# Front of a decoder-layer kernel: weight chunks begin beside x on a second queue, and the 80-column product moves behind the first group

## The reference

```
h    = rms_norm(x, attn_norm_g)
proj = h @ w_in                       # (256, 2048) @ (2048, 11344)
(q_sb, k_sb, v_sb, q_ds, k_ds, v_ds, q_ix, k_ix, w_ix, g_sb, g_ds) = split(proj)
```

## Time and profile before

| what | value |
|---|---|
| median of 3 runs | 1457.61 us |
| the profiled execution's own time | 1458.54 us |
| its span, first to last instruction | 1456.6 us |
| PE busy | 1444.3 us (99%) |
| DVE busy | 1025.4 us (70%) |
| ACT busy | 799.1 us (55%) |
| GpSimd busy | 431.1 us (30%) |
| moved by DMA | 272.12 MB, mean 187 GB/s |

### The profile page before, as it was taken

The page is one execution under the profiler, slowest core; times in us unless marked ns, Lnnn a source line. Parts: engine busy times, 40 slices in busy tenths (PEclk is TensorE's granted clock), DMA queues, the critical chain, the costliest instruction groups (busy, mean ns, idle before and its releaser), DMA issues.

```text
span 1456.6 us, 24290 instructions
## 1 busy us (share of the span) xinstructions
PE 1444.3 (99%) x7640; PEld 1236.5 (85%) x7640; DVE 1025.4 (70%) x1352; ACT 799.1 (55%) x1107; POOL 431.1 (30%) x486
## 2 busy tenths in 40 slices
PE   8999999999999999999999999999999999999998
PEld 6888888888888888888888888888888888788887
DVE  6545455886655556775557778777777778899987
ACT  6544445565766756665455454545554545455553
POOL 1100000323222223450005556655556555200000
PEclk9999999999999999999999999999999999999999
DMA  7666665666555555575666666666666665576664
GB/s 244 194 182 187 182 179 172 188 178 183 147 171 164 153 168 176 188 245 183 192 175 187 188 190 186 181 192 199 190 187 180 194 189 187 173 242 205 196 209 145
DMA packets 130493, 272.12 MB, mean 187 GB/s; under 512 B 10784, under 2 KB 10816, under 8 KB 130192
## 3 DMA queue, kind: packets, MB, share of 16 engines
q1 hardware_dynamic: 129664, 269.12, 60.2%
q0 software_dynamic: 464, 2.42, 0.5%
q10 hardware_dynamic: 320, 0.01, 0.0%
HBM read 269.42 MB, written 2.10 MB: 186 GB/s over the span
## 4 chain that ended last, share of the span: by engine, by line
PE 95%; DVE 2%; POOL 1%; issue 1%; DMA 1%; ACT 0%; DVEq 0%; ACTq 0%; POOLq 0%; SPq 0%
PE bank L1640 94%; DVE lo L1239 1%; PE bank L1689 0%; POOL u L1604 0%; DMA rows_in<-in_attn_norm_g 0%; DMA raw<-in_w_down 0%; POOL conv L1607 0%; PE bank L1823 0%; DVE conv L1193 0%; DVE y L1329 0%; PE bank L1863 0%; POOL conv L1621 0%; DVE leftb L1308 0%; DVE hT L907 0%; ACT hi L820 0%
## 5 line engine op out<-in xcount | busy, mean ns | idle before, releaser
L882 DVE TENSOR_TENSOR lo<-raw,hi 128x1024 fp32r<-128x1024 f32 (+1 forms) x423 | 545.2, 1293 | 314.3 <-ACT hi L511 313.5
L511 ACT ACTIVATE hi<-raw 128x1024 fp32r<-128x1024 f32 (+1 forms) x423 | 445.5, 1055 | 408.2 <-PE bank L1640 403.4
L1640 PE MATMUL bank<-h2T,hi 128*128 128x512 f32 x1408 | 483.3, 394 | 0.0
L1640 PE MATMUL bank<-h2T,lo 128*128 128x256 f32 x1408 | 376.6, 278 | 0.0
L1640 PEld LDWEIGHTS bank<-h2T,hi 128*128 128x128 f32 x1408 | 257.9, 188 | 53.6
L1640 PE MATMUL bank<-hT,hi 128*128 128x512 f32 (+1 forms) x784 | 273.3, 394 | 0.7 <-DVE lo L882 0.7
L1640 PEld LDWEIGHTS bank<-h2T,lo 128*128 128x128 f32 x1408 | 264.5, 188 | 7.8
L1640 PE MATMUL bank<-hT,lo 128*128 128x256 f32 (+1 forms) x784 | 214.7, 284 | 0.0
L1640 PE MATMUL bank<-hi,hT 128*128 128x512 f32 x640 | 198.0, 390 | 0.0
L1604 POOL TENSOR_TENSOR u<-u,rms_row 128x256 f32<-128x256 f32 x88 | 121.0, 1375 | 239.7 <-DVE u L1183 220.7
L1640 PE MATMUL bank<-hi,ffT 128*128 128x512 f32 x576 | 177.6, 390 | 2.1 <-DVE lo L1239 2.1
(11 more groups left out here) (223 smaller groups left out, 1574.9 us busy)
## 6 DMA issues: line engine op xcount, KB each, us to landing
raw<-in_w_in SPq DMA_DIRECT2D x176, 512.0 KB, 3.6
raw<-in_w_up SPq DMA_DIRECT2D x176, 512.0 KB, 3.8
raw<-in_w_down SPq DMA_DIRECT2D x88, 512.0 KB, 4.3
raw<-in_w_branch SPq DMA_DIRECT2D x32, 512.0 KB, 3.6
raw<-in_w_out SPq DMA_DIRECT2D x32, 512.0 KB, 3.8
y<-in_x SPq DMA_DIRECT2D x4, 512.0 KB, 6.7
y<-in_x POOLq DMA_DIRECT2D x1, 2048.0 KB, 9.4
out<-y SPq DMA_DIRECT2D x8, 256.0 KB, 3.6
```

The lines of the kernel that those rows point to most:

```text
L511: act.activation(hi[s][:, 0:width], raw[s][:, 0:width], ACT.Copy)\
L882: dve.tensor_tensor(lo[s][:, 0:width], raw[s][:, 0:width], hi[s][:, 0:width].bitcast(f32), ALU.subtract)\
L1640: return pe.matmul(o, l, r, start=start, stop=stop, skip_group_check=True)
```

## The change

1. SP issues no x and no 80-column loads. It begins with the first large chunks; its waits are satisfied for the first four, since DVE, PE and ACT raise `lo_done`, `w_used` and `hi_done` by 4 in advance (and SP itself `w_landed`).
2. x comes on ACT's queue, in four column quarters of two loads each (256 KB a load, 8 loads), issued behind the gain. The positions are loaded by GpSimd.
3. The first group's product starts when k tiles 0 and 1 of x and the first chunk are there. The other transposes of x are inserted behind chunks 0 to 5, two k tiles at a time, and so are their copies on ACT and DVE, the four squares on ACT and the five parameter transposes.
4. The 80 columns get own buffers (`wtail`, `wtail_hi`, `wtail_lo`), are loaded by GpSimd in four pieces, converted in two halves at (g, j) = (0, 6) and (0, 7), and multiplied after chunk 7 into bank B[2], behind `spread_rms`. The small work behind it moves to later j.
5. `rows_in` is no longer zeroed (only the rows that are loaded are read). The identity is ready before the other patterns, PE waits for it alone, and it does 11 idle transposes in place of 14.

The diff, cut to what these points touch:

```diff
@@ SP
-            for half in range(2):
-                cols = slice(half * BLOCK, (half + 1) * BLOCK)
-                for t in range(TH):
-                    sp.dma_start(y[:, t, cols], x[0, t * P:(t + 1) * P, cols])\
-                        .then_inc(x_in[2 * half + t], 16)
...
+            for s in range(SLOTS):
+                sp.sem_inc(w_landed[s], 16)
@@ ACT
-            act.wait_ge(rows_zero, 1)
+            prime(act, relu_done, tok_done, tok_done, *[hi_done] * C_ROWS)
             act.dma_start(rows_in[0:KT, 0, :], attn_norm_g.rearrange("(t p) -> t p", p=P))\
                 .then_inc(small_in, 16)
+            for q in range(4):
+                for t in range(TH):
+                    cols = slice(q * GRP, (q + 1) * GRP)
+                    act.dma_start(y[:, t, cols], x[0, t * P:(t + 1) * P, cols])\
+                        .then_inc(x_in[2 * q + t], 16)
...
+            transposed_hi(hT, 0, 0, range(0, 2))
             split(C_ROWS)
+            transposed_hi(hT, 0, 0, range(2, 4))
             split(C_ROWS + 1)
             split(C_ROWS + 2)
+            transposed_hi(hT, 0, 0, range(4, 6))
...
+                            if g == 0 and j < 5:
+                                transposed_hi(hT, 0, 0, range(2 * j + 6, 2 * j + 8))
+                            if g == 0 and 1 <= j < 5:
+                                squares((j - 1) // 2, (j - 1) % 2)
...
+                            if (g, j) == (0, 6):
+                                tail_split(0)
                                 norm_rstd(0)
+                            if (g, j) == (0, 7):
+                                tail_split(1)
+                                act.wait_ge(rstd_done, 1)
+                            if (g, j) == (1, 0):
+                                rms_copy(0)
+                            if (g, j) == (1, 1):
+                                act.wait_ge(angle_done, 1)
+                                act.activation(trig[:, :, :, :], ang[:, :, :, :], ACT.Sin)\
+                                    .then_inc(sin_done, 1)
+                                act.wait_ge(tail_prod, 1)
+                                act.activation(tailT[0:TAIL, :], B[2][0:TAIL, S:2 * S], ACT.Copy)\
+                                    .then_inc(tailT_half, 1)
@@ DVE
+                        if not index and (g, j) == (0, 5):
                             dve.wait_ge(const_sel, 2)
                             mean_squares(0, 2)
+                        if not index and (g, j) == (0, 6):
+                            tail_split(0)
+                        if not index and (g, j) == (0, 7):
+                            tail_split(1)
                             rms_diagonal(0)
...
@@ GpSimd
-            pool.memset(rows_in[:, :, :], 0.0).then_inc(rows_zero, 1)
...
+            for c in range(4):
+                rows = w_in[c * 4 * P:(c + 1) * 4 * P, TAIL_AT:TAIL_AT + TAIL]
+                pool.dma_start(wtail[:, 4 * c:4 * c + 4, :],
+                               rows.rearrange("(k p) c -> p k c", p=P)).then_inc(tail_in, 16)
@@ PE
-            pe.wait_ge(const_sel, 2)
-            keep_warm(14)
+            pe.wait_ge(const_sel, 1)
+            keep_warm(11)
...
+            x_transposes(range(0, 4))
...
+            def tail_product():
+                pe.wait_ge(tail_lo, 2)
+                for kt in range(KT):
+                    mm(B[2][0:TAIL, :], wtail_hi[:, kt, :], hT[:, kt, :], kt == 0, False)
+                    i = mm(B[2][0:TAIL, 0:S], wtail_lo[:, kt, :], hT[:, kt, 0:S], False,
+                           kt == KT - 1)
+                i.then_inc(tail_prod, 1)
...
+                        if not index and g == 0:
+                            pe.wait_ge(xT_lo, CK * (j + 1))
                         rows_chunk(C_ROWS + g * CPG + j + 1 + 2 * CPG * b, j % SLOTS, hT,
...
+                            if g == 0 and j < 6:
+                                x_transposes(range(2 * j + 4, 2 * j + 6))
+                            if (g, j) == (0, 4):
+                                other_params()
+                            if (g, j) == (0, 7):
+                                spread_rms(0)
+                                tail_product()
+                            if (g, j) == (1, 1):
                                 pe.wait_ge(tailT_done, 1)
```

More of the change, by code:

```diff
@@ L274, in hybrid_layer @@
         w_used = sem("w_used")
-        x_in = [sem(f"x_in{i}") for i in range(2 * TH)]
+        x_in = [sem(f"x_in{i}") for i in range(4 * TH)]
         pos_in = sem("pos_in")
@@ L543, in squares @@
             def squares(half, t):
-                act.wait_ge(x_in[2 * half + t], 16)
+                for q in (2 * half, 2 * half + 1):
+                    act.wait_ge(x_in[2 * q + t], 16)
                 act.activation(junk[:, t, half * BLOCK:(half + 1) * BLOCK],
@@ L554, in _, with tail_split @@
             act.wait_ge(params_done, 1)
-            for c in range(C_ROWS):
-                transposed_hi(hT, 0, 0, range(TAIL_CK * c, TAIL_CK * (c + 1)))
-                split(c, width=TAIL_CK * TAIL)
-                if c == 1:
-                    squares(0, 0)
+            transposed_hi(hT, 0, 0, range(0, 2))
             split(C_ROWS)
-            squares(0, 1)
+            transposed_hi(hT, 0, 0, range(2, 4))
             split(C_ROWS + 1)
-            squares(1, 0)
             split(C_ROWS + 2)
-            squares(1, 1)
-            act.wait_ge(params_T, 2)
-            act.activation(params[:, KT:2 * KT + 8 * FT], A[3][:, KT:2 * KT + 8 * FT],
-                           ACT.Copy).then_inc(params_done, 1)
-            act.wait_ge(w_used, C_ROWS)
-            act.activation(tailT[0:TAIL, :], A[2][0:TAIL, S:2 * S], ACT.Copy)\
-                .then_inc(tailT_half, 1)
+            transposed_hi(hT, 0, 0, range(4, 6))
+            def tail_split(h):
+                act.wait_ge(tail_in, 16 * 4)
+                kts = slice(h * KT // 2, (h + 1) * KT // 2)
+                act.activation(wtail_hi[:, kts, :], wtail[:, kts, :], ACT.Copy)\
+                    .then_inc(tail_hi, 1)
             def rows_body(b, index):
@@ L1735, in _, with x_transposes @@
-            pe.wait_ge(conv_in, 16 * 3)
-            pe.wait_ge(params_done, 1)
-            pe.transpose(A[3][:, KT:2 * KT], rows_in[0:KT, 1, :], ident[0:KT, 0:KT])
-            for k in range(4):
-                at_ = 2 * KT + 2 * FT * k
-                i = pe.transpose(A[3][:, at_:at_ + 2 * FT], rows_in[0:2 * FT, 2 + k, :],
-                                 ident[0:2 * FT, 0:2 * FT])
-            i.then_inc(params_T, 1)
+            def x_transposes(kts):
+                for t in range(TH):
+                    pe.wait_ge(x_in[2 * (kts[0] // 4) + t], 16)
+                transposes(0, kts, y)
@@ new lines, in _, with other_params @@
+            x_transposes(range(0, 4))
[6 more added lines that the diff above has]
+                i.then_inc(tail_prod, 1)
+            def other_params():
+                pe.wait_ge(conv_in, 16 * 3)
+                pe.wait_ge(params_done, 1)
+                pe.transpose(A[3][:, KT:2 * KT], rows_in[0:KT, 1, :], ident[0:KT, 0:KT])
+                for k in range(4):
+                    at_ = 2 * KT + 2 * FT * k
+                    i = pe.transpose(A[3][:, at_:at_ + 2 * FT], rows_in[0:2 * FT, 2 + k, :],
+                                     ident[0:2 * FT, 0:2 * FT])
+                i.then_inc(params_T, 1)
```

115 lines of the change are left out of this document (51 added, 64 removed).

## The result

The changed kernel takes 1465.57 us (median of 6 runs, 1464.23 to 1466.14) beside 1457.53 for the kernel before in the same runs (1457.03 to 1458.03): ratio 1.0054 [1.0043, 1.0065], 8.0 us slower. Forecast were 1462.1 us and a range from 1458.8 to 1465.2. The direction and the two waits behind the first group were right; the size was wrong by 3.5 us. The profiled execution has a span of 1463.7 and a time of 1465.47 us.

What follows compares the result with a forecast made beforehand. PE's own time was taken as the bound, busy 1444.3 of 1456.6 us. Terms -0.1 + 3.2 + 0.9 + 0.5 = +4.5 us on the median 1457.6 gave 1462.1, with 8 in 10 between 1458.8 and 1465.2.

Steps and rivals of the forecast that it cites:

- the two waits behind the first group: New PE waits ahead of spread_rms, 3.2 us, and for tailT behind the second group's chunk 1, 0.9 us.
- The method of the sum: To the end of b = 0: gain is 11.1 us less the first large product's start; new waits are added.
- When the first large product starts: Front: first transpose of x at 7.3, first large product at 11.0 us, bounds 9.9 and 12.5; worth 0.1 us.
- no second path to memory: Front loads: queues of several engines share the same 16 DMA engines, so a second queue saves issuing time only.
- The clock: PE's front: slow state at 11.0 us would cost 1.6 us, plus 0.4 for transposes; left to a rival.
- Slow clock: Rival at the first chunk: PE at its low clock level adds 2.0 us, giving 1464.1; chance 0.20.
- late x: Rival in the front: x and weights starve each other, first product at 12.5, weights' wait 2, giving 1465.1; chance 0.09.
- 1/rms: Ahead of spread_rms behind chunk 7: PE waits 3.2 us for DVE's chain to diag, between 2.5 and 3.8.
- `tailT`: Behind the second group's chunk 1: PE waits 0.9 us for ACT's copy and DVE's sum, from 0.5 to 1.2.
- no idle time behind b = 0: Nothing after b = 0 takes the loss back, since PE has no idle time there that could shrink.
- Weights in the first group: Around chunk 3 of the first group: PE waits 0.5 us for converted weights, bounds 0 and 2.

Runs made afterwards that it cites:

- experiment 12: Experiment 11 with 15 idle transposes at the start in place of 11; 1456.92 us, ratio 0.9993 to the kernel before.
- experiment 4: Changed kernel with all of x on SP's queue, a quarter ahead of each chunk of weights, ACT issuing the gain alone; 1466.93 us.
- experiment 10: Changed kernel with only GpSimd's four tail loads held back until chunk 2 is converted; 1465.31 us.
- experiment 3: Changed kernel with x's first quarter issued by SP ahead of its weights, the rest of x on ACT; 1468.09 us.
- experiment 1: Changed kernel with 26 more idle transposes behind the transposed gain, to fill PE's pause until x lands; 1465.97 us.
- experiment 2: Changed kernel with spread_rms and the 80-column product behind chunk 8, and the small work behind them one chunk later; 1461.66 us.
- experiment 5: Changed kernel with x and weights all on SP in order of need, and tail loads issued once chunk 2 is converted; 1463.77 us.
- experiment 6: Experiment 5 with 16 idle transposes between x's first transposes and chunk 0; 1462.22 us.
- experiment 7: Experiment 6 with experiment 2's shift and tailT copied before the sines; 1457.4 us, ratio 0.9999 to the kernel before.
- experiment 8: Changed kernel, loads unchanged, with 26 idle transposes ahead of x's first transposes and 16 behind them; 1465.6 us.
- experiment 9: Experiment 7 with GpSimd's five small parameter loads held back until chunk 0 is converted; 1457.67 us.
- experiment 11: Experiment 9 with the two loads of the positions also held back, behind the five parameter loads; 1457.4 us.

## Why the prediction was wrong

**The method of the sum held.** That the moved work is only moved, so that the change is worth 11.1 us less the start of the first large product, plus new waits: the found terms add to 8.1 of 8.31. In experiment 12 the same account gives 10.27 - 11.1 + 0.41 = -0.4, and with the 0.2 left over above -0.2; the point moved from 76.11 to 75.94.

**When the first large product starts: failed, 12.50 for 11.0.** Both halves of the step were set too low. x landed at 2.22 + 6.20 = 8.4, not at 7.1. The kernel moved 94 GB/s in its first 5 us, where the kernel before moved 180 and where the step took half of 290 from 2.7 us on. x's first load is issued at 1.75 us on ACT, against 0.81 on SP before, and PE's first transpose of x starts 6.8 us behind that issue; in experiment 4, with x first on SP's queue and issued at 0.81, it starts 4.9 us behind it. The first chunk of weights was issued late too, at 1.63, behind the semaphores that the engines now raise in advance. The sum had no term for that, and no run shows what it did to x. ACT was ready at 8.6, not 7.2: eight loads of x cost 0.68 us each, where I took 0.52 from two loads of the positions. By the step's own terms ACT at 8.6 gives 8.6 + 0.8 + 1.07 + 1.23 + 0.1 = 11.8 and the transposes at 8.55 give 8.55 + 3.7 = 12.25; the rest comes from these transposes, slow at 1.94 us, so that ACT's first copy starts 0.77 us behind the first of them in place of 0.54. So x decided, and experiment 10 agrees, where ACT was ready 0.8 us sooner for nothing. That there is no second path to memory was right: in experiment 3 x was there 2.9 us sooner and chunk 0 only at 12.1, in experiment 4 chunks 1 and 2 came at 14.4 and 18.6 in place of 12.9 and 17.5. The Trainium skill, "DMA: Bandwidth & Descriptors", "Issuing engines are not separate DMA queues", adds that a second engine saves issuing time, "which is usually small relative to the DMA itself". Here nothing was saved: issuing on ACT cost 5.4 us ahead of ACT's first work.

**The clock: failed, and this is the larger part.** The cost was priced (2.0, found 2.8) but stood in the sum at nothing and in a rival at 0.20. The argument against it, that the engine stayed fast over idle time in 5 to 15 us, was drawn from rows in which PE's longest pause between 5 and 15 us was about 1 us; the new pauses were 3.82 and 2.01, and I had forecast both, as about 3 and 2.6. The Trainium skill, "TensorE: Matmul & The Clock Gate", "What's actually happening", has the low level as the default, and the trace agrees: in the changed kernel everything from the first idle transpose to chunk 0 ran low. Chunk 0 ran low behind pauses of 2.0 to 7.0 us in the changed kernel and experiments 1 to 5 and 10, and high in 6 to 9, 11 and 12, where a fill stood in the pause. In experiment 1 alone had the engine been at the upper level before the pause; there the clock fell, and in the others it had not yet risen. How much of the low level is owed to the pause and how much to the little work ahead of it the runs separate in experiment 1 only.

**Rivals taken as alternatives.** Slow clock and late x were set against each other, each with its own time (1464.1, 1465.1), though nothing keeps both from happening; a late x even lengthens the pause. Together, by the text's own numbers but without the wait for weights that a slow chunk 0 hides: 4.5 + 1.5 + 2.0 - 0.5 = 7.5, or 1465.1. That joint case had no chance of its own, and the range ended at 1465.2.

**1/rms and `tailT`: right** (3.2 and 3.12; 0.9 and 0.78), by the row of DVE work that the step listed: it ended at 43.8. Not foreseen is what the longer wait does to the product behind it, 0.9 to 1.6 us in 6 of 8 profiles. The statement that PE has no idle time behind b = 0 missed the 2.1 us of waits for `lo` that the kernel before has from 90 us on; at the point compared here they play no part.

**Weights in the first group: right in its place, hidden.** Chunk 2 was the late one, and it would have cost 2.5 us (experiment 8); the slow chunk 0 lay over it. The forecast had it as a term of 0.5 that adds to the others; it is one of two that overlap, 2.5 us under the 2.8 of the clock.

Open are: whether the changed kernel's runs at 0.998 and 0.999 paid in the 80-column product, as experiment 5 suggests; whether the positions or chance delayed chunk 0 in experiment 9; and why PE waits once or twice for `lo` late in the program.

## What to carry to other kernels

Work that is moved from before the first product to behind it gains nothing by itself: count only the idle time that goes, and then price each new pause of TensorE twice, once for its length and once for the low clock that may follow it. Two delays that overlap (a slow chunk, late weights) must be removed together: either removal alone gained next to nothing here (experiments 8 and 10). Put the loads of a front in one queue in the order in which they are needed, and keep issues off an engine whose first work is waited for: with x there at 5.7, ACT's first copy started at 7.25 behind six issues (experiment 3) and at 6.45 behind none (experiment 4).

## What the runs showed of the hardware

- TensorE's clock fell behind a wait of 3.1 us that came about 40 us into the kernel, behind 16 us or more of unbroken matmuls, in 6 of 8 profiles, and cost the next product 0.9 to 1.6 us. I had looked for the lower level only at the program's start. Other waits left it up: 2.10 us in experiment 8, 1.11 and 1.45 in experiment 4.
- The granted-clock column misses some of these: 1.00 in the changed kernel while pairs of 512-column matmuls took 1.06 in place of 0.62 us; 0.83 in experiment 5. The durations of like matmuls are the surer sign.
- Issuing a load cost ACT 0.52 us in the kernel before (two of 0.5 KB), 0.68 in the changed kernel (eight of 256 KB) and 0.58 in experiment 10, the same eight with GpSimd's four tail loads held back; SP's four weight loads took 2.77 us in the changed kernel and 3.14 in experiment 3.
- A 512 KB chunk landed within about 5.7 us of its issue in experiment 12, and in a median of 10.1 us for those of the changed kernel's first 20 us, in which 5.3 MB moved.
